# A routed mixture-of-experts block on one Trainium2 core: the router's logits computed with stationary weights, its decisions taken on logits, and the work around the router reordered

## The reference

```
lg  = xt @ w_rg + b_rg                      # 4 group logits per token
grp = argmax(lg);  p_grp = softmax(lg)[grp]
le  = (xt @ w_re + b_re)[group grp]         # 8 expert logits of that group
top_p, top_i = top_k(softmax(le), 2)
gate = top_p / sum(top_p) * p_grp
y = sum over the token's 2 experts e: gate * ((silu(x @ w_eg[e]) * (x @ w_eu[e])) @ w_ed[e])
```

## Time and profile before

| | us |
|---|---|
| median of 3 runs | 1918.65 |
| profiled execution | 1915.69 |
| its span | 1913.8 |
| PE busy in the span | 1816.0 (95%) |
| DVE busy | 973.5 (51%) |
| ACT busy | 684.9 (36%) |
| DMA over the span | 483.46 MB, mean 253 GB/s |

### The profile page before, as it was taken

One profiled execution on the slowest core, in us unless ns is written; L12 is line 12 of the kernel. 1 busy time (PEld: TensorE's weight loads), 2 busy tenths in 40 slices (PEclk: granted clock), 3 DMA queues, 4 the chain that ended last, 5 costly groups with the idle time before them and its releaser, 6 DMA issues.

```text
span 1913.8 us, 33015 instructions
## 1 busy us (share of the span) xinstructions
PE 1816.0 (95%) x13763; PEld 1487.7 (78%) x13763; DVE 973.5 (51%) x1406; ACT 684.9 (36%) x1051; POOL 21.3 (1%) x14
## 2 busy tenths in 40 slices
PE   7999989999999998999998999999979999999997
PEld 5999979999899986799997899888864543443443
DVE  3988669886865445355455876477431111111111
ACT  3444454444444425344444533466311110110101
POOL 0000000000000000000000111000000000000000
PEclk9999999999999999999999999999979999999999
DMA  9998529986574512344541333533356999999997
GB/s 388 425 375 339 218 79 363 351 336 255 199 292 170 197 56 88 117 188 169 197 167 65 132 108 114 206 108 127 133 198 256 413 425 426 425 424 425 425 426 296
DMA packets 46044, 483.46 MB, mean 253 GB/s; under 512 B 5104, under 2 KB 5232, under 8 KB 7152
## 3 DMA queue, kind: packets, MB, share of 16 engines
q1 hardware_dynamic: 44496, 476.09, 62.9%
q10 hardware_dynamic: 1440, 5.77, 0.8%
HBM read 480.79 MB, written 1.05 MB: 252 GB/s over the span
## 4 chain that ended last, share of the span: by engine, by line
PE 41%; DMA 9%; DVE 4%; ACT 2%; issue 1%; DVEq 0%; SPq 0%; ACTq 0%
PE psG L398 25%; DMA ring<-stream 9%; PE psA L398 9%; PE psS L398 6%; DVE mem L2422 1%; PE psS L1321 0%; DVE parts L2108 0%; DVE mem L2192 0%; ACT mem L1532 0%; ACT parts L1521 0%; PE psA L994 0%; DVE mem L2680 0%; DVE mem L2420 0%; DVE X L2201 0%; PE psS L1174 0%
## 5 line engine op out<-in xcount | busy, mean ns | idle before, releaser
L398 PE MATMUL psG<-parts 128*128 128x256 f32 x6016 | 765.1, 285 | 10.1 <-DVE parts L2108 5.7
L398 PEld LDWEIGHTS psG<-parts 128*128 128x128 f32 x6016 | 739.2, 193 | 30.6 <-issue 19.2
L398 PE MATMUL psA<-parts 128*128 128x256 f32 x2368 | 303.2, 284 | 1.8 <-DVE parts L2279 1.6
L398 PEld LDWEIGHTS psA<-parts 128*128 128x128 f32 x2368 | 290.7, 192 | 18.1 <-issue 15.6
L398 PE MATMUL psS<-ring,mem 128*64 128x512 f32 (+1 forms) x1028 | 231.3, 595 | 21.4 <-DMA ring<-stream 17.9
L2046 DVE TENSOR_TENSOR parts<-ring,parts 128x2048 fp32r<-128x2048 f32 x80 | 183.1, 2289 | 117.6 <-ACT parts L1497 117.3
L398 PEld LDWEIGHTS psS<-ring,mem 128*64 128x64 f32 (+1 forms) x1028 | 72.0, 137 | 176.4 <-issue 129.6
L1497 ACT ACTIVATE parts<-ring 128x2048 fp32r<-128x2048 f32 x80 | 153.1, 1914 | 89.1 <-PE psA L398 88.4
L2037 DVE SCALAR_TENSOR_TENSOR mem<-ring,silc,mem 128x1536 f32<-128x1536 f32 (+1 forms) x98 | 138.8, 1417 | 2.5
L2267 DVE TENSOR_TENSOR mem<-mem,psS 128x512 f32<-128x512 f32 x16 | 11.0, 687 | 234.1 <-ACT mem L1950 234.1
L2108 DVE TENSOR_TENSOR parts<-ring,parts 128x1024 fp32r<-128x1024 f32 x76 | 92.9, 1230 | 59.5 <-ACT parts L1521 58.1
(11 more groups left out here) (356 smaller groups left out, 1527.0 us busy)
## 6 DMA issues: line engine op xcount, KB each, us to landing
ring<-stream SPq DMA_DIRECT2D x300, 1536.0 KB, 8.9
mem<-stream ACTq DMA_DIRECT2D x9, 512.0 KB, 7.8
X<-x_in SPq DMA_DIRECT2D x1, 1024.0 KB, 17.8
ring<-stream SPq DMA_DIRECT2D x1, 1024.0 KB, 22.3
mem<-masks ACTq DMA_DIRECT2D x1, 1024.0 KB, 4.8
x_out<-X SPq DMA_DIRECT2D x4, 256.0 KB, 2.9
ring<-stream SPq DMA_DIRECT2D x1, 512.0 KB, 23.4
cst<-consts SPq DMA_DIRECT2D x1, 304.0 KB, 2.9
```

The lines of the kernel that those rows point to most:

```text
L398: return nc.tensor.matmul(out, lhsT, rhs, start=start, stop=stop, skip_group_check=True)
```

## The change

It has four parts. (1) In the start, `rest_ada` moves on PE behind `first_gate_up`, `turn_rest` behind `gate_up(0, 1)`; the copy between them moves behind `high_down(0, 1)` on ACT, the sum that uses them into the loop of `ffn` on DVE, and SP loads the rest of chunk 5 after chunk 7 in place of after chunk 6. (2) SP issues the early weights, after the last norm's sums and ahead of the chunk that waits for the router's own. (3) The router's logits are computed with the 36 columns stationary and 256 tokens moving, even and odd k on partitions 0 to 35 and 64 to 99 of `psS`; DVE and ACT copy the two partial sums to SBUF and one matmul per half of the tokens adds and transposes them (against `FO`, made by `orders` ahead of the norm with the constants of `first_max`). The 16 transposes stand between these matmuls, and 22 filler matmuls behind them. The decisions are taken on logits; only the five differences per token half that the gates need are exponentiated. (4) `selection`, `gather` and `xe` of the first pair stand ahead of the branch, and the gates are computed in between. Positions are now 1-based against an `iota` that starts at 1.

```diff
-                if n == RING:
+                if n == RING + 1:
                     sp.dma_start(ring[:, RING - 1, SLOT:CHUNK], stream[RING - 1, :, SLOT:CHUNK])\
...
+            for n in range(whole, BASE["out"] + 2 + RING):
...
+            sp.wait_ge(sem("pre_sum"), 8)
+            for i, b in enumerate(EARLY_AT):
+                sp.dma_start(blk(b), stream[NCHUNK + i // 3, :, (i % 3) * SLOT:(i % 3 + 1) * SLOT])\
+                    .then_inc(sem("early_in"), 16)
...
                 first_gate_up()
                 if layer == 0:
+                    rest_ada()
+                gate_up(0, 1)
+                if layer == 0:
                     turn_rest()
-                gate_up(0, 1)
                 down(0, 0, first=True)
             def router():
...
+                for k in range(KT):
+                    pe.wait_ge(h_ready, 8 * 7 + k + 1)
+                    a, r = 2 * SLOT + k * 36, 64 * (k % 2)
+                    last = mm(psS[r:r + 36, 0, 0:S], chunk(c, a, a + 36), H[:, k, :], start=(k < 2), stop=(k >= KT - 2))
+                    if k % 2 == 1 and k < KT - 1:
+                        token(0, k - 1)
+                        token(0, k)
+                last.then_inc(chunk_used, 1)
+                for k in (KT - 2, KT - 1):
+                    token(0, k)
+                for k in range(3):
+                    token(1, k)
+                pe.wait_ge(sem("rt_lgx"), 1)
+                pe.wait_ge(sem("rt_lgy"), 1)
                 for t in range(TT):
-                    for k in range(KT):
-                        pe.wait_ge(h_ready, 8 * 7 + k + 1)
-                        a = 2 * SLOT + k * 36
...
+                last.then_inc(sem("rt_lgt"), 1)
+                for k in range(3, KT):
+                    last = token(1, k)
                 last.then_inc(sem("rt_htok"), 1)
+                idle(22, P)
                 pe.wait_ge(sem("rt_asg"), 1)
...
+                mm(psS[:, 1, 0:E], before, ASG[:, 0, :], start=True, stop=True)
+                mm(psS[:, 1, E:2 * E], before, ASG[:, 1, :], start=False, stop=False)
+                mm(psS[:, 1, E:2 * E], ones, ASG[:, 0, :], start=False, stop=True).then_inc(sem("rt_cnt"), 1)
+                idle(4, P)
+                pe.wait_ge(sem("htok_out"), 1)
+                gather_half(0, 0, 0)
                 pe.wait_ge(sem("rt_max1"), 1)
-                nc.tensor.transpose(psS[0:1, 0, 256:256 + P], blk(22)[:, 128:129], ident).then_inc(sem("rt_max1t"), 1)
+                nc.tensor.transpose(psS[0:1, 0, 0:P], blk(22)[:, 128:129], ident).then_inc(sem("rt_max1t"), 1)
...
+                        gather_half(r, p + 1, 1)
                     down(r, p)
-                pe.wait_ge(sem("htok_out"), 1)
-                gather(0, 0)
+                pe.wait_ge(sem("rt_gate"), 1)
                 select(0, 0)
                 step(0, 0)
...
                         high_down(0)
+                        high_down(0, 1)
                         ac.wait_ge(chunk_used, 6)
-                        A(ADR[:, 768:1024], psA[:, 2, 0:S], ACT.Copy).then_inc(sem("ada_row"), 1)
-                        high_down(0, 1)
+                        A(ADRN, psA[:, 2, 0:S], ACT.Copy).then_inc(sem("ada_row"), 1)
                     elif layer < 3:
                         high_down(layer, 1)
...
                 tick(72)
             def router():
+                ac.wait_ge(chunk_used, BASE["out"] + 3)
+                A(LGX[64:100], psS[64:100, 0, 0:S], ACT.Copy).then_inc(sem("rt_lgy"), 1)
+                A(blk(24)[0:1, 1000:1001], eps[0:1, 0:1], ACT.Exp)
                 ac.wait_ge(sem("rt_htok"), 1)
                 A(HTOK.rearrange("p t (b n) -> p (t b) n", b=2), psA[:, :, :], ACT.Copy).then_inc(sem("htok_out"), 1)
                 ac.wait_ge(sem("rt_max"), 1)
-                A(blk(24)[:, 256:264], blk(24)[:, 256:264], ACT.Exp)
-                A(blk(24)[:, 128:192], blk(24)[:, 128:192], ACT.Exp).then_inc(sem("rt_exp"), 1)
+                A(EX, EX, ACT.Exp).then_inc(sem("rt_exp"), 1)
             def sparse():
...
-            for i, b in enumerate(EARLY_AT):
-                nc.scalar.dma_start(blk(b), stream[NCHUNK + i // 3, :, (i % 3) * SLOT:(i % 3 + 1) * SLOT])\
-                    .then_inc(sem("early_in"), 16)
...
                 add_acc()
...
+            def orders():
+                for i in range(32):
+                    V.memset(blk(24)[:, 584 + i:585 + i], float(32 - i))
+                for i in range(4):
+                    V.memset(blk(24)[:, 576 + i:577 + i], float(4 - i))
+                V.memset(LGX[32:64], 0.0)
+                link(V.tensor_tensor(FO, ident[:, 0:36], ident[:, 64:100], ALU.add))
...
+                ve.wait_ge(sem("rt_lgt"), 1)
+                lg = psS[:, 0, S:S + 72].rearrange("p (t c) -> p t c", t=2)
...
-                    o4 = OH[:, t, :][:, :, None].to_broadcast([P, 4, 8])
-                    le = LGT[:, t, 4:36].rearrange("p (g e) -> p g e", g=4)
...
-                link(V.tensor_reduce(Z[:, 2], EXL, AX.X, ALU.add))
-                first_max(LE, W32, O1, 3, 32)
...
+                    last = V.tensor_tensor(LE[:, t, :].rearrange("p (g e) -> p g e", g=4),
+                                           lg[:, t, 4:36].rearrange("p (g e) -> p g e", g=4),
+                                           OH[:, t, :][:, :, None].to_broadcast([P, 4, 8]), ALU.add)
+                link(last)
+                first_max(LE, W32, O1, 1, 32)
+                link(V.scalar_tensor_tensor(T1, O1, -4e30, LE, ALU.mult, ALU.add))
                 first_max(T1, W32, O2, 4, 32)
                 link(V.tensor_tensor(ASG, O1, O2, ALU.add), "rt_asg")
-                link(V.tensor_tensor(Z[:, 5], Z[:, 3], Z[:, 4], ALU.add))
-                link(V.tensor_tensor(Z[:, 5], Z[:, 5], Z[:, 2], ALU.mult))
+                V.tensor_tensor(EXL, lg[:, :, 0:4], Z[:, 0].to_broadcast([P, 2, 4]), ALU.subtract)
+                link(V.tensor_tensor(D2, Z[:, 4], Z[:, 1], ALU.subtract), "rt_max")
+                ve.wait_ge(sem("rt_cnt"), 1)
+                link(V.tensor_tensor(POS, ASG, psS[:, 1, 0:2 * E].rearrange("p (t e) -> p t e", t=2), ALU.mult))
+                selection(0, 0)
+                link(V.tensor_reduce(blk(22)[:, 128:129], blk(22)[:, 64:128], AX.X, ALU.max), "rt_max1")
...
+                ve.wait_ge(sem("rt_exp"), 1)
+                link(V.tensor_reduce(Z[:, 2], EXL, AX.X, ALU.add))
+                link(V.scalar_tensor_tensor(Z[:, 5], D2, 1.0, Z[:, 2], ALU.add, ALU.mult))
                 link(V.reciprocal(Z[:, 5], Z[:, 5]))
-                link(V.tensor_tensor(Z[:, 3], Z[:, 3], Z[:, 5], ALU.mult))
-                link(V.tensor_tensor(Z[:, 4], Z[:, 4], Z[:, 5], ALU.mult))
-                link(V.tensor_tensor(O1, O1, Z[:, 3].to_broadcast([P, 2, 32]), ALU.mult))
-                link(V.tensor_tensor(O2, O2, Z[:, 4].to_broadcast([P, 2, 32]), ALU.mult))
+                V.tensor_tensor(O1, O1, Z[:, 5].to_broadcast([P, 2, 32]), ALU.mult)
+                link(V.tensor_tensor(Z[:, 3], D2, Z[:, 5], ALU.mult))
+                link(V.tensor_tensor(O2, O2, Z[:, 3].to_broadcast([P, 2, 32]), ALU.mult))
                 link(V.tensor_tensor(G3, O1, O2, ALU.add), "rt_gate")
-                ve.wait_ge(sem("rt_cnt"), 1)
-                link(V.tensor_tensor(POS, ASG, psS[:, 0, 0:2 * E].rearrange("p (t e) -> p t e", t=2), ALU.mult))
-                link(V.tensor_reduce(blk(22)[:, 128:129], blk(22)[:, 64:128], AX.X, ALU.max), "rt_max1")
-                link(V.tensor_scalar(POS, POS, -1.0, None, ALU.add))
...
                 ve.wait_ge(sem("rt_max1t"), 1)
-                link(V.tensor_reduce(blk(22)[0:1, 130:131], psS[0:1, 0, 256:256 + P], AX.X, ALU.max))
                 link(V.tensor_copy(most[0:1, 0:1], blk(22)[0:1, 130:131]), "rt_flag")
+                xe(0, 0, 1)
             V.memset(eps[:, :], EPS)
             ve.wait_ge(sem("cols_in"), 16)
...
                                         ALU.add, ALU.mult))
             pre_norm(0, 0)
-            ve.wait_ge(sem("ada_rest"), 1)
-            mod_out(0, 16, 2)
```

140 lines of the change are left out of this document (68 added, 72 removed).

## The result

The kernel after took 1901.93 us (median of 8 runs, 1899.72 to 1908.90), the kernel before 1918.18 in the same comparison (8 runs, 1913.34 to 1920.49). The ratio is 0.9925, with a 95% interval of 0.9911 to 0.9938: 14.4 us less, 11.9 to 17.1. Over all runs made for this study, the kernel before has a mean of 1916.9 (51 runs) and the kernel after 1903.9 (19 runs): 13.1 us less.

What follows compares the result with a forecast made beforehand. The expert loop was taken as bound by the weight stream, whose start waits for PE's router path. Router -10.7 and start -0.6 gave -11.3 us, so 1918.65 became 1907.4, range 1904.6 to 1912.5.

Steps and rivals of the forecast that it cites:

- Router: Path from the last norm's H to the first expert matmul: that matmul at 1430.7 instead of 1441.38, 10.7 us earlier.
- PE's branch: Router step behind the gather: taken as 1.06 us, DVE's value, as the trace showed only 0 to 2.26 for PE.
- low for part of the way: Router rival: clock stays low for a stretch, costing 1.9 us or twice that, 1909.2 to 1911; chance 0.20.
- The drains: Router: eight tiling-mode switches, each costing a 0.21 us tail, 1.7 us at most, giving 1909.1; chance 0.05.
- The start: First feed-forward block and moved multiplication: `down(0, 0)` at about 50.1 instead of 50.74, 0.6 us gained.
- my sign of being wrong: Start: the prediction called itself wrong if, among other signs, `first_gate_up` ended later than 43.
- The stream follows PE: Expert loop: fixed length from the first expert matmul, so the end moves one for one with that start.
- The rival that nothing arrives: Expert loop: the stream ends the kernel whatever PE does, none of the 10.7 us arrives, 1918 stands; chance 0.07.
- the last line of the sum: Whole kernel: 11.3 us taken off the median of the runs before, 1918.65 - 11.3 = 1907.4.
- the better case's two terms: No clock drop at the start (1.1 us more) and a shorter PE branch (0.5 to 1): 1905.3; chance 0.12.
- two low stretches with the drains: Upper end of the range: clock low at two router places plus the tiling-switch drains, put at 1912.5.

Runs made afterwards that it cites:

- e4: Kernel before with filler matmuls alone added behind router matmuls, before the counts and behind the maximum's transpose; 1911.97 us, ratio 0.9968.
- e7: Kernel after with the first pair's selection, gather and copy put back behind the branch; 1907.87 us, ratio 0.9962.
- e5: Kernel after without the 22 fillers between the router's transposes and the counts; 1906.07 us, ratio 0.9945.

## Why the prediction was right in kind and too small

- **Router.** Forecast 10.7, measured 11.5 in each of the three profiles of the whole change (H to E 17.57 or 17.58). Relative to the first H block, the forecast put the partial sums' copies at 3.91, the decision chain at 5.06, the assignment at 9.76, the counts at 10.76, the gather's end at 16.4 and the expert matmul at 18.4. Measured: 4.38, 5.65, 10.24, 10.87, 16.55, 17.57. The first half was up to 0.6 late. The fillers stand behind it and so began late too, 5.96 behind H in place of 5.46, but the 44 instructions took 4.91 in place of 5.30: my price of 0.1205 held a share of its group's tail. **The mis-sized term of the sum is PE's branch:** I took DVE's 1.06 inside a bound of 0 to 2.26; the gap on PE was 0.32. The flag was written at 1425.11, 0.74 ahead of the end of the gather; that its being there already is what makes PE's branch short is likely, but no run shows it. `select` took 0.70 in place of 0.9. A still shorter branch would bring little: the second half of `xe` ends at 1426.64, and PE began 0.22 behind it in e4 and e7, which gives 1426.86, the time that was measured.
- **The clock at the router.** That it would stay up was right, in every profile of the new router with 18 or 22 fillers. The rival "low for part of the way" did not occur.
- **The drains.** I had read from the earlier trace rows that a switch of tile size costs nothing, and gave the rule 0.05. In after, two router matmuls and two transposes come in 0.56 + 0.37 us in the chain of waits:

```profile
1410.85 0.37 PE psA L1254 x2
1411.21 0.56 PE psS L415 x4
```

At 0.107 an instruction (half of 0.2145) they would be 0.43 + 0.21, so by this estimate a pair of switches costs 0.29, 0.15 each; no run takes the switches away by themselves. The Trainium skill, "TensorEngine Tiling (Array Packing)", Tiling Modes / Key Properties, says that a change of tiling mode drains the engine; the 0.29 us agree with it, though at 1460 us nothing of it can be seen. The copies of the partial sums began 0.47 us later than forecast, and most of that is likely this. It passed on to the fillers, whose lower price made up for it.
- **The start.** Forecast 0.6. From the first H block to the next norm's it is 220.10 to 220.13 us in the four profiles with the old order, and 219.75 in the mean of the ten with the new (219.04 to 220.88): 0.4. Where the granted clock falls equally far behind H, it is 0.56 (220.13 in before, 219.57 in e7). So the size was about right, but my sign of being wrong came true: `first_gate_up` ended at 44.11, later than 43, and `down(0, 0)` began at 51.26 in place of 50.1. Of both, 0.97 is the first H block, which came later; counted from it they are 0.4 and 0.2 late. What I had not seen is that this H block itself moves by 4 us between executions: it comes at 30.33 to 31.87 in nine profiles, at 32.81 to 33.16 in the four whose clock falls at 23 to 24 us, and at 34.57 in one with a fall at 29.6.
- **The stream follows PE.** Right: 464.39 us of loop in both. The rival that nothing arrives is refuted.
- **What made the number wrong.** The stages give 11.52 + 0.45, that is 12.0 us, inside my range of 6.2 to 14.1. The measured median was 16.7 below the three runs from which I started. Of the 4.7 between, 1.6 is the base: those three runs had 1918.65, all 51 have 1917.0. One more is the first eight runs of after (1901.93; all 19 have 1902.9). Another is the median, which leaves out what the slower executions add: of the 19 runs of after, 14 lie between 1899.7 and 1904.0 and five between 1907.2 and 1910.4, so from 1917.0 to 1902.9 are 14.1 by the medians, but 13.1 by the means (standard error 0.8; 12.5 by the sum of the parts' means, 1.4 for the start's runs and 11.1 for the router's). The last 1.1, from 12.0 to 13.1, may be chance.

**The step that failed is thus the last line of the sum and the range around it.** I took a median of three runs as the base and put the clock falls of the untouched code at nothing. They are up to 3.4 us of lost clock at one place, shift an execution's untouched stretch by up to 5 us, and move even a median of eight by 1. The profile of before showed three of them (820, 1096, 1318) beside the one at the start and the one at the router, and I priced only the last two; I had even noted that the profiled execution ran 3.0 below the median, and drew nothing from it. PE's branch and `select`, 0.9 us too dear together, are the smaller part. The range was also added up wrongly: the better case's two terms in full give 1905.3, not 1904.6, and two low stretches with the drains 1912.9, not 1912.5.

The falls explain the scatter, and with it the first three pieces, 3.6 us together, and most of the 3.5 us between the two first profiles. They do not explain the last 1.1 us: by the mean granted clocks of all runs that have one, before lost 25.7 us of clock an execution, of which 12.0 at the router (half of 23.9, as in its profile), and after 13.3, so outside the router the two differ by 0.4 us of lost clock, or 0.2 us of time.

How the router's 11.52 us divide: 4.2 is what fillers alone bring to the old order (e4), 2.9 the first pair ahead of the branch (e7). The remaining 4.4, the shorter chain on logits, the exponentials out of its way and the earlier logits, are a difference only; no run took that part alone. Since e4's clock fell once more ahead of the gather, the clock's share in the old order is at least that 4.2. It depends on the order, though: in the new one, taking the 22 fillers away costs 0.88 (e5).

## What to carry to other kernels

Where a decision chain stands ahead of a stream that has run full, price the chain from the last input to the first instruction that frees a buffer; here all of it arrived at the end, and the stream's own length did not matter. Fillers sized to end with the wait they cover were worth it, and a few too many cost most of their excess: compare the end of the fillers with the end of the result that they cover. And before calling a time wrong or right by a few microseconds, count the clock falls in the profile of before: they belong in the range, and a base of three runs is a thin one (here 1.6 us off).

## What the runs showed of the hardware

- Falls of the clock to the 1.2 GHz level cost the same program a different amount in each execution. The lost clock between 280 us and the router was 3.4, 5.1, 6.8, 8.5 or 11.9 us in 14 profiles, at seven places (696, 720, 820, 1026, 1100, 1238, 1320 us), of which each execution has a subset; the price is about 0.54 us per us lost.
- A branch on a loaded value cost PE 0.32 us behind a gather, where the flag had been written 0.7 us before; DVE's, straight behind the flag that it wrote itself, cost 1.06 and 1.06 again in e7.
- Fillers of 128 columns ran at 0.1116 us each when back to back (44 in 4.91 us), less than the 0.1205 I had taken from a group of 18 with its tail.
